# The odd mixer's operations in another order: scan beside value jobs, key copy in pieces, copies ahead of exponentials, turns in two banks

## The chip, the cores and the metric

One core of a Trainium2 chip runs the whole program. Times are device microseconds from start to end of one execution. TensorE (PE) multiplies, VectorE (DVE), ScalarE (ACT) and GpSimd (POOL) work on elements, and SyncE (SP) issues most of the DMAs. Every engine runs its own list of instructions in order, and semaphores alone order the engines against each other.

## The reference, cut to what matters

The program is a two-layer image-like block, then a two-layer sequence block on 512 tokens of width 1024, all in fp32: an even mixer, a feed-forward part, an odd mixer, a feed-forward part. The change lies in the odd mixer. It has two halves that do not depend on each other until the output product:

```python
def s5_group(u, ...):                      # 32 groups, 64 complex states
    bu = einsum('bsgh,gph->bsgp', u, b_bar)
    state = associative_scan(s5_combine, (a_bar, bu))   # h = a*h + b, over time
    y = gelu(real(einsum('bsgp,ghp->bsgh', state, cm)) + d_skip * u)
    return y * sigmoid(y @ w_glu + b_glu)

def mla_group(c_q, c_kv, k_rope, pos, ...):             # 8 heads
    q = (rms_norm(c_q) @ w_uq).reshape(b, s, 8, 64 + 32)   # 32 of them rotated
    kv = (rms_norm(c_kv) @ w_ukv).reshape(b, s, 8, 64 + 64)
    k_rot = rope(k_rope)                   # one for all 8 heads
    p = softmax((q_nope @ k_nope + q_rot @ k_rot) * scale, causal by chunks of 64)
    return p @ v
```

## The kernel before, in words

All of it is one straight program for each engine. For the odd mixer one list, `odd_program` (L336), gives the order of the jobs, and TensorE (L1687 on), ScalarE (`odd_mixer`, L2270 on) and VectorE (L3220 on) each walk this same list and do their own share of each job. So the list is the order of work on three engines at once.

The jobs: `uq i` multiplies the normalised query rank by the weights of head i (6 matmuls, L1313), ScalarE copies the 96 rows to `qm` (L2280). `swap i` multiplies head i by a permutation (L1701) into bank 5, and VectorE rotates the head with three operations (L3228 to L3230). `k7` makes the kernels of the S5 steps with 64 matmuls of 16 columns (L1705). `wt i` transposes four blocks of 128 by 128 (L1709), ScalarE copies them (L2282). `kn i` makes the unrotated key of head i, `v i` 128 tokens of values. `in i` feeds 8 groups of the S5 input through the transposed blocks (L1725). `rot1 i` and `rot2 i` are one matmul (L1732) and three VectorE operations each, ahead of and behind the scan (L3250), which VectorE does in one instruction after `rot1 3`. `out`, `ytr`, `glu` finish S5.

`unit u` is attention for one head and one query tile of 128 (32 units, a pair of heads side by side). In slot u of the list TensorE does the scores of unit u (L1646, banks 0 and 1 in turn), the turn of unit u-2 (transposes of the probabilities, L1656, into bank 4), and in even slots the product with the values (mix, L1669). VectorE does the maximum of unit u and the weighting of unit u-1. ScalarE does the exponential of unit u (L2253) and then the copy of the turned probabilities of unit u-2 (L2261). A turn waits for its weighted probabilities and for the copy of the turn ahead of it, since both use bank 4. An exponential waits for its maximum and for the turn of unit u-2. A copy waits for its turn and for the mix that last read its buffer. Scores of unit u wait for the exponential of unit u-2. From unit 28 on parts of the output product (`early`) stand between the units.

All the jobs other than the swaps and units use banks 2 and 3 in turn, and wait until the job two places ahead has been taken out of its bank.

Ahead of the mixer stands the input product (`od_in`, L1609): ten tiles of 24 matmuls, which VectorE takes out and between which it computes the S5 tables (`tables`, L3141). TensorE's swap of the key rope part (L1630) stands behind tile 6. VectorE's key rope (L3179 to L3181) stands behind the scaling of the query rank. At the end of this part VectorE copies the rotated key part to all 8 heads of `km` in one instruction (L3187). TensorE enters the mixer when the variance of the kv rank has been computed (L3155).

Of the kernel before, what the change touches and what calls it, by code (L numbers as in the profile page):

```python
# [335 lines left out]
def odd_program():  # L336

    some = lambda kind, *which: [(kind, i) for i in which]
    program = some("uq", 0, 1) + some("swap", 0) + some("uq", 2) + some("swap", 1) + some("uq", 3) + some("swap", 2)
    program += some("k7", 0) + some("wt", 0) + some("swap", 3) + some("wt", *range(1, 8))  # L340
    program += some("kn", *range(4)) + some("v", *range(4)) + some("in", *range(4))
    beside = {0: some("rot1", 0, 1), 1: some("rot1", 2, 3), 2: some("uq", 4), 3: some("uq", 5) + some("swap", 4), 4: some("uq", 6) + some("swap", 5),
              5: some("uq", 7) + some("swap", 6), 6: some("rot2", 0, 1) + some("swap", 7), 7: some("rot2", 2, 3), 8: some("kn", 4, 5), 9: some("kn", 6, 7),
              11: some("out", 0, 1), 12: some("out", 2, 3), 13: some("out", 4, 5), 14: some("out", 6, 7), 16: some("ytr", 0, 1), 17: some("ytr", 2, 3),
              20: some("glu", 0), 21: some("glu", 1), 22: some("glu", 2), 23: some("glu", 3)}
    for u in range(35):
        program += some("unit", u) + beside.get(u, []) + some("early", *range(2 * (u - EARLY_AT), 2 * (u - EARLY_AT) + 2) if u >= EARLY_AT else ())
    return program


SIDE = [item for item in odd_program() if item[0] in SIDE_BY]


# [17 lines left out]
def build(nc, xt, ctxt, cvec, pack1, pack_c, w_fnet, w_ada, w_in, w_br, w_merge, w_out,  # L371
          pos, pack2, s5_bc, ev_w_in, ev_w_out, od_w_in, w_glu, w_uq, w_ukv, od_w_out, ffn_gate, ffn_up, ffn_down, out):
    ctx = ExitStack()
    with ctx:
# [292 lines left out]
        od_ready = sem("od_ready")  # L667
        odd_done = sem("odd_done")
# [4 lines left out]
        kr_swapped = sem("kr_swapped")  # L673
# [231 lines left out]
        def _(pe):  # L905
# [703 lines left out]
            def od_in():  # L1609
                q0 = PANEL0["od_in"]  # L1610

                def sums(name, k_tiles, bank, freed):
                    pe.wait_ge(od_ready, freed)
                    for k in range(k_tiles):
                        pe.wait_ge(squared, NORM0[name] + k + 1)
                        mm(psum[:, bank * BANK:(bank + 1) * BANK], ones2, NORM_AT[name][0][:, k, :], start=k == 0, stop=k == k_tiles - 1).then_inc(summed, 1)

                for n, tile in enumerate(OD_TILES):
                    if n % 2 == 0:
                        w = split_ready(q0 + n // 2)  # L1620
                    if n >= 7:
                        pe.wait_ge(od_ready, max(1, n - 7))
                    split_job(n % 8, w, tile % 2 * P if tile < 9 else 64, h2_parts, each=norm_tile(4) if n == 0 else None).then_inc(gemm_done, 1)
                    if n == 0:
                        statistics("mix1")
                    if n == 5:
                        sums("q", 3, 2, 3)
                    if n == 6:
                        pe.wait_ge(od_ready, 6)
                        mm(psum[64:96, 4 * BANK:5 * BANK], c2("swap_mla")[64:96, 64:96], kr[64:96, :], start=True, stop=True).then_inc(kr_swapped, 1)  # L1630
                    if n == 7:
                        sums("kv", 2, 3, 4)

            def odd_mixer():
# [4 lines left out]
                def scores(u):  # L1639
                    h, i = units[u]  # L1640
                    pe.wait_ge(qm_roped, h + 1)
                    pe.wait_ge(side_freed["act"], side_evicted("kn", h))
# [6 lines left out]
                def turn(u):  # L1649
                    h, i = units[u]  # L1650
                    pe.wait_ge(p2_weighted, u0 + u + 1)
                    if u:
                        pe.wait_ge(p2T_ready, u0 + u)
                    for j in range(i + 1):
                        o = 4 * BANK + j * P
                        last = nc.tensor.transpose(psum[:, o:o + P], pr_mla[0][:, u % 2, j * P:(j + 1) * P], ident2)  # L1656
                    last.then_inc(turned2, 1)
# [28 lines left out]
                for what, i in odd_program():  # L1686
# [15 lines left out]
                    elif what == "k7":  # L1702
                        pe.wait_ge(wv_ready, 1)
# [3 lines left out]
                    elif what == "wt":  # L1707
                        for g in range(4):
# [84 lines left out]
        def _(act):  # L1793
# [449 lines left out]
            def odd_mixer():  # L2243
# [12 lines left out]
                def copy(u):  # L2256
# [4 lines left out]
                    f(pr_mla[1][:, u % 2, 0:n], psum[:, 4 * BANK:4 * BANK + n], ACT.Copy).then_inc(p2T_ready, 1)  # L2261
# [8 lines left out]
                for what, i in odd_program():  # L2270
# [8 lines left out]
                    if what == "uq":  # L2279
                        f(qm[0:96, i, :], src[0:96, :], ACT.Copy).then_inc(side_freed["act"], 1)  # L2280
                    elif what == "wt":
# [15 lines left out]
                    elif what == "unit":  # L2297
                        if i < len(units):
                            exps(i)
                        if 0 <= i - 2 < len(units):  # L2300
                            copy(i - 2)
# [29 lines left out]
        def _(dve):  # L2331
# [784 lines left out]
            def od_in():  # L3116
# [49 lines left out]
                for n in range(10):  # L3166
# [7 lines left out]
                    elif n == 7:  # L3174
                        low_rank_scale("q", cq, "q_norm")
                        dve.wait_ge(kr_swapped, 1)
# [4 lines left out]
                        order(tt(kr[p], kr[p], temp, ALU.add))  # L3181
# [5 lines left out]
                order(v.tensor_copy(km[64:96], kr[64:96].unsqueeze(1).broadcast_to([32, MLAH, SEQ])))  # L3187

            def odd_mixer():
# [29 lines left out]
                for what, i in odd_program():  # L3219
# [5 lines left out]
                    if what == "swap":  # L3225
                        r = slice(0, 96)
                        dve.wait_ge(qm_swapped, i + 1)
# [74 lines left out]
        def _(pool):  # L3302
# [74 lines left out]
            for t in range(4):  # L3377
                pool.wait_ge(od_ready, 7 + t)
# [189 lines left out]
```

## Time and profile before

| | us |
|---|---|
| median of 3 runs (lowest, highest) | 2979.51 (2977.66, 2985.71) |
| the profiled execution, its own time | 2982.23 |
| its span, first to last instruction | 2980.3 |
| TensorE busy | 2870.1 (96%) |
| VectorE, GpSimd, ScalarE busy | 1405.7, 1356.8, 851.6 |
| share of TensorE in the chain that ended last | 83% |

The span is what the profile sees; the execution's own time has 1.93 us more around it. A time in a row counts from the start of the span. The odd mixer lies at about 2352 to 2558.

### The profile page before, as it was taken

The numbers are of one execution on the slowest core, as the hardware profiler recorded it, in microseconds if no ns is written. First come the engines' busy times: TensorE is split into PE (matmuls) and PEld (weight loads), VectorE is DVE, ScalarE is ACT, GpSimd is POOL, SyncE is SP. The second block draws the span as 40 slices with busy tenths as digits, with TensorE's granted clock in tenths as the row PEclk, the third lists the DMA queues.
The fourth block names the chain that finished last, engine by engine and source line by source line (L and its number), as shares of the span: only waits on it lengthen the run. The fifth ranks groups of instructions, "written<-read, shape, count | busy, mean of one in ns | idle before, by whom it ended". The sixth has DMA issues, their size and how long they took to land.

```text
span 2980.3 us, 36560 instructions
## 1 busy us (share of the span) xinstructions
PE 2870.1 (96%) x14468; PEld 2202.2 (74%) x14468; DVE 1405.7 (47%) x2280; ACT 851.6 (29%) x1579; POOL 1356.8 (46%) x1106
## 2 busy tenths in 40 slices
PE   8999999999989999999999998999999888999997
PEld 5878777777878777677876666788787545788886
DVE  3311656766563123436755876525536854611113
ACT  3011432320130143323245243232233124322222
POOL 2334323223535544458754544744445211744443
PEclk9999999999999999999999999999999899999999
DMA  7112222223312212133211112323324200323322
GB/s 279 44 43 64 64 70 90 65 93 124 102 43 85 78 53 71 54 127 103 85 59 56 57 43 75 98 85 89 105 76 149 59 30 29 108 90 92 106 82 74
DMA packets 244820, 245.76 MB, mean 82 GB/s; under 512 B 5376, under 2 KB 234624, under 8 KB 244032
## 3 DMA queue, kind: packets, MB, share of 16 engines
q1 hardware_dynamic: 243360, 239.92, 25.2%
q0 software_dynamic: 1312, 3.80, 0.4%
q8 instruction: 101, 1.65, 0.2%
q14 instruction: 47, 0.39, 0.0%
HBM read 235.19 MB, written 7.34 MB: 81 GB/s over the span
## 4 chain that ended last, share of the span: by engine, by line
PE 83%; DVE 13%; ACT 2%; issue 1%; SPq 1%; POOL 0%; DMA 0%; DVEq 0%; ACTq 0%; POOLq 0%
PE psum L930 22%; PE psum L932 21%; PE psum L931 21%; PE psum L1196 4%; PE psum L1313 1%; PE psum L1175 1%; PE psum L1131 1%; DVE columns L2610 1%; PE psum L1086 1%; PE psum L1151 1%; PE psum L1130 1%; PE psum L1200 1%; PE psum L1386 1%; DVE columns L2881 1%; PE psum L1462 1%
## 5 line engine op out<-in xcount | busy, mean ns | idle before, releaser
L930 PE MATMUL psum<-columns,columns 128*128 128x512 f32 (+1 forms) x3464 | 1350.6, 390 | 13.2 <-POOL columns L3320 5.0
L932 PE MATMUL psum<-columns,columns 128*128 128x512 f32 (+1 forms) x3464 | 1265.3, 365 | 0.0
L931 PE MATMUL psum<-columns,columns 128*128 128x512 f32 (+1 forms) x3464 | 1263.1, 365 | 0.0
L3320 POOL TENSOR_TENSOR columns<-columns,columns 128x512 fp32r<-128x512 f32 (+1 forms) x676 | 912.2, 1380 | 436.3 <-ACT columns L1850 403.1
L3316 POOL TENSOR_TENSOR columns<-columns,columns 128x512 fp32r<-128x512 f32 x392 | 418.3, 1098 | 1066.3 <-PE psum L932 835.6
L930 PEld LDWEIGHTS psum<-columns,columns 128*128 128x128 f32 x3464 | 656.0, 189 | 194.9 <-issue 76.0
L931 PEld LDWEIGHTS psum<-columns,columns 128*128 128x128 f32 x3464 | 656.6, 190 | 125.6 <-issue 29.2
L932 PEld LDWEIGHTS psum<-columns,columns 128*128 128x128 f32 x3464 | 654.9, 189 | 111.7
L1850 ACT ACTIVATE columns<-columns 128x1024 fp32r<-128x1024 f32 (+2 forms) x154 | 136.8, 936 | 170.1 <-PE psum L932 165.8
L2610 DVE SCALAR_TENSOR_TENSOR columns<-columns,columns,columns 128x256 f32<-128x256 f32 x224 | 153.7, 740 | 0.0
L2592 DVE SCALAR_TENSOR_TENSOR columns<-columns,psum 128x512 f32<-128x512 f32 x80 | 54.7, 684 | 185.8 <-PE psum L1196 183.4
L2988 DVE TENSOR_TENSOR columns<-columns,psum 128x512 f32<-128x512 f32 x44 | 30.3, 689 | 207.2 <-PE psum L932 207.2
L1196 PE MATMUL psum<-columns,columns 128*128 128x512 f32 x256 | 120.4, 592 | 1.4 <-DVE columns L2569 1.4
L2982 DVE TENSOR_TENSOR columns<-psum,columns 128x512 f32<-128x512 f32 x44 | 30.4, 692 | 151.8 <-PE psum L932 151.5
L2551 DVE TENSOR_REDUCE columns<-psum 128x1 f32<-128x768 f32 (+3 forms) x80 | 61.5, 769 | 64.7 <-PE psum L1131 63.6
L3104 DVE TENSOR_TENSOR psum<-psum,columns 128x512 f32<-128x512 f32 x32 | 22.4, 700 | 129.2 <-PE psum L932 129.1
L1959 ACT ACTIVATE columns<-psum,columns 128x768 f32<-128x768 f32 (+3 forms) x80 | 59.4, 742 | 71.6 <-DVE columns L2554 71.5
L2189 ACT ACTIVATE columns<-columns 128x512 fp32r<-128x512 f32 x44 | 27.9, 633 | 179.0 <-DVE columns L2988 179.0
L1974 ACT ACTIVATE columns<-psum 128x512 f32<-128x512 f32 (+1 forms) x80 | 44.1, 551 | 113.4 <-PE psum L1151 113.4
L2000 ACT ACTIVATE columns<-psum,columns 128x512 f32<-128x512 f32 x64 | 43.7, 682 | 111.6 <-PE psum L932 111.5
L1966 ACT ACTIVATE columns<-columns,columns 128x768 f32<-128x768 f32 (+3 forms) x80 | 62.6, 783 | 45.2 <-DVE columns L2562 45.1
L2185 ACT ACTIVATE columns<-columns 128x512 f32<-128x512 f32 x44 | 27.8, 632 | 162.0 <-DVE columns L2982 161.8
(410 smaller groups left out, 2859.9 us busy)
## 6 DMA issues: line engine op xcount, KB each, us to landing
columns<-in_w_merge SPq DMA_DIRECT2D x32, 1024.0 KB, 6.3
columns<-in_w_ada SPq DMA_DIRECT2D x24, 1024.0 KB, 5.3
columns<-in_w_in SPq DMA_DIRECT2D x22, 1024.0 KB, 5.3
columns<-in_ev_w_in SPq DMA_DIRECT2D x22, 1024.0 KB, 5.2
columns<-in_ffn_gate SPq DMA_DIRECT2D x22, 1024.0 KB, 5.3
columns<-in_ffn_up SPq DMA_DIRECT2D x22, 1024.0 KB, 5.3
columns<-in_ffn_down SPq DMA_DIRECT2D x16, 768.0 KB, 4.7
columns<-in_ffn_down SPq DMA_DIRECT2D x16, 640.0 KB, 4.3
```

Of the source, the lines that this page charges most:

```text
L930: mm(dst, weights(0, k), moving(0, k), start=start and k == 0, stop=False)
L931: mm(dst, weights(0, k), moving(1, k), start=False, stop=False)
L932: last = mm(dst, weights(1, k), moving(0, k), start=False, stop=stop and k == k_tiles - 1)
L1196: last = mm(psum[:, o:o + SEQ], brs[:, n % 2, k, part * P:(part + 1) * P], gx[:, r, k, :], start=k == 0, stop=k == 1)
L1850: last = f(w_parts[0][:, (SPLITS[q] - 1) % 2, a:b], ring[:, raw_slot, a:b], ACT.Copy)
L1959: f(prob[:, u % 2, 0:n], psum[:, o:o + n], ACT.Exp, bias=cols[:, u % 2:u % 2 + 1], scale=0.125, accum_out=cols[:, 4 + u % 2:5 + u % 2]).th ...
L1966: f(prob[:, u % 2, 0:n], prob[:, u % 2, 0:n], ACT.Identity, scale=cols[:, 24 + u % 8:25 + u % 8]).then_inc(prob_weighed, 1)
L2551: order(v.tensor_reduce(top, psum[:, o:o + n], AX.X, ALU.max))
L2592: v.scalar_tensor_tensor(out=acc if j < quarter else g, in0=g, scalar=1.0, in1=y, op0=ALU.add, op1=ALU.mult).then_inc(merge_used, 1)
L2610: last = v.scalar_tensor_tensor(out=acc, in0=w, scalar=sil[:, k, b:b + 1], in1=acc, op0=ALU.mult, op1=ALU.add)
L3316: last = g.tensor_tensor(high[:, c], raw[:, c], zero.broadcast_to([P, c.stop - c.start]), ALU.add)
L3320: last = g.tensor_tensor(low[:, c], raw[:, c], high[:, c].bitcast(F32), ALU.subtract)
```

## The change

Seven edits, none of which adds or removes arithmetic:

- The list of jobs is written anew. Six of the eight transpose jobs stand among the first `uq` and `swap` jobs, ahead of `k7`; the other two, `swap 3` and the `in` jobs follow it. `kn` and `rot1` alternate, and the `v` jobs stand behind the last `rot1`, beside the scan. Units 0 to 3 have one `uq` and one `rot2` beside them, units 4 to 7 one `swap` and one `kn`, units 8 to 10 nothing. From unit 11 on the list is as it was.
- The key rope's swap on TensorE stands behind tile 7 instead of tile 6.
- The copy of the key part to 8 heads is taken from VectorE and made by ScalarE in four pieces of 32 by 1024, each behind one of the copies `uq` 0 to 3. Scores wait for their piece (`km_ready`).
- ScalarE's copy of unit u-2 stands ahead of the exponential of unit u.
- Turns from unit 9 on use banks 4 and 5 in turn, and wait for the copy two turns ahead.
- The wait for the S5 tables moves from `k7` to `wt 0`.
- Semaphore counts follow from these.

```diff
-    program = some("uq", 0, 1) + some("swap", 0) + some("uq", 2) + some("swap", 1) + some("uq", 3) + some("swap", 2)
-    program += some("k7", 0) + some("wt", 0) + some("swap", 3) + some("wt", *range(1, 8))
-    program += some("kn", *range(4)) + some("v", *range(4)) + some("in", *range(4))
-    beside = {0: some("rot1", 0, 1), 1: some("rot1", 2, 3), 2: some("uq", 4), 3: some("uq", 5) + some("swap", 4), 4: some("uq", 6) + some("swap", 5),
-              5: some("uq", 7) + some("swap", 6), 6: some("rot2", 0, 1) + some("swap", 7), 7: some("rot2", 2, 3), 8: some("kn", 4, 5), 9: some("kn", 6, 7),
+    program = some("uq", 0, 1, 2) + some("swap", 0) + some("uq", 3) + some("wt", 0, 1) + some("swap", 1) + some("wt", 2, 3, 4, 5)
+    program += some("swap", 2) + some("k7", 0) + some("wt", 6, 7) + some("swap", 3) + some("in", *range(4))
+    for n in range(4):
+        program += some("kn", n) + some("rot1", n)
+    program += some("v", *range(4))
+    beside = {0: some("uq", 4) + some("rot2", 0), 1: some("uq", 5) + some("rot2", 1), 2: some("uq", 6) + some("rot2", 2),
+              3: some("uq", 7) + some("rot2", 3), 4: some("swap", 4) + some("kn", 4), 5: some("swap", 5) + some("kn", 5),
+              6: some("swap", 6) + some("kn", 6), 7: some("swap", 7) + some("kn", 7),
...
+TURNS_APART = 9
+def turn_bank(u):
+    return 4 + (u % 2 if u >= TURNS_APART else 0)
...
+        km_ready = sem("km_ready")
...
-        kr_swapped = sem("kr_swapped")
...
-                    if n == 6:
+                    if n == 7:
...
-                        mm(psum[64:96, 4 * BANK:5 * BANK], c2("swap_mla")[64:96, 64:96], kr[64:96, :], start=True, stop=True).then_inc(kr_swapped, 1)
-                    if n == 7:
+                        mm(psum[64:96, 4 * BANK:5 * BANK], c2("swap_mla")[64:96, 64:96], kr[64:96, :], start=True, stop=True).then_inc(qm_swapped, 1)
...
+                    pe.wait_ge(km_ready, h // 2 + 1)
...
+                    if u == TURNS_APART:
+                        pe.wait_ge(qm_roped, MLAH)
...
-                        pe.wait_ge(p2T_ready, u0 + u)
+                        pe.wait_ge(p2T_ready, u0 + u - (u > TURNS_APART))
...
-                        o = 4 * BANK + j * P
+                        o = turn_bank(u) * BANK + j * P
...
-                        pe.wait_ge(wv_ready, 1)
...
+                        if i == 0:
+                            pe.wait_ge(wv_ready, 1)
...
-                    f(pr_mla[1][:, u % 2, 0:n], psum[:, 4 * BANK:4 * BANK + n], ACT.Copy).then_inc(p2T_ready, 1)
+                    o = turn_bank(u) * BANK
+                    f(pr_mla[1][:, u % 2, 0:n], psum[:, o:o + n], ACT.Copy).then_inc(p2T_ready, 1)
...
+                        if i == 0:
+                            act.wait_ge(od_ready, 9)
+                        if i < 4:
+                            f(km[64:96, 2 * i:2 * i + 2], kr[64:96].unsqueeze(1).broadcast_to([32, 2, SEQ]), ACT.Copy).then_inc(km_ready, 1)
...
+                        if 0 <= i - 2 < len(units):
+                            copy(i - 2)
...
-                        if 0 <= i - 2 < len(units):
-                            copy(i - 2)
...
-                        dve.wait_ge(kr_swapped, 1)
+                        dve.wait_ge(qm_swapped, 1)
...
-                        order(tt(kr[p], kr[p], temp, ALU.add))
+                        tt(kr[p], kr[p], temp, ALU.add).then_inc(od_ready, 1)
+                        dve.wait_ge(od_ready, 9)
...
-                order(v.tensor_copy(km[64:96], kr[64:96].unsqueeze(1).broadcast_to([32, MLAH, SEQ])))
...
-                        dve.wait_ge(qm_swapped, i + 1)
+                        dve.wait_ge(qm_swapped, i + 2)
...
-                pool.wait_ge(od_ready, 7 + t)
+                pool.wait_ge(od_ready, 7 + t + t // 2)
...
```

## Rows read from the trace of the kernel before

**Rows 1.** The page: the span.
```profile
span 2980.3 us, 36560 instructions
```

**Rows 2.** Busy us by stretch: PE, PEld, DVE, ACT, POOL; then PEclk, DMA share, GB/s.
```profile
2410.00:2468.00 58.00, 44.79 (x145) 19.64 (x146) 40.87 (x90) 14.76 (x38) 7.77 (x9) 0.88 0.13 40
...
2558.00:2620.00 62.00, 61.47 (x260) 48.73 (x261) 34.06 (x31) 18.62 (x27) 48.01 (x36) 1.00 0.33 103
```

**Rows 3.** Whom TensorE waited for from 2325 to 2558 (total us, times, longest).
```profile
PE psum L1656 <- ACT columns L2261: 20.6, 10, 5.8
...
PE psum L1630 <- DVE columns L3136: 3.7, 1, 3.7
PE psum L1732 <- DVE columns L3243: 2.2, 3, 1.1
```

**Rows 4.** TensorE in order of time: start us, us, what (L1313 products, L1701 swaps).
```profile
2352.24 5.31 PE L1313 MATMUL psum<-columns,columns 128*96 128x512 f32 x12
2357.39 1.02 PE L1701 MATMUL psum<-columns,columns 96*96 96x512 f32 x2
2358.25 2.74 PE L1313 MATMUL psum<-columns,columns 128*96 128x512 f32 x6
2365.47 1.99 PE L1701 MATMUL psum<-columns,columns 96*96 96x512 f32 x2 [4.47 <-DVE columns L3230]
2367.25 4.54 PE L1313 MATMUL psum<-columns,columns 128*96 128x512 f32 x6
```

**Rows 5.** VectorE in order of time: variance of kv, copy of keys, scan.
```profile
2350.36 0.68 DVE L3155 TENSOR_SCALAR columns<-psum 128x512 f32<-128x512 f32 x1
...
2360.87 2.28 DVE L3187 COPY columns<-columns 32x4096 f32<-32x4096 f32 x1
...
2420.83 4.42 DVE L3250 TENSOR_TENSOR_SCAN columns<-columns,columns 128x2048 f32<-128x2048 f32 x1
```

**Rows 6.** TensorE in order of time, units 1 to 11 (L1646 scores, L1656 turns).
```profile
2417.95 2.82 PE L1313 MATMUL psum<-columns,columns 128*96 128x512 f32 x6 [0.99 <-DVE columns L3243]
...
2427.00 0.45 PE L1656 MATMUL psum<-columns,columns 128*128 128x128 f32 x1 [5.80 <-ACT columns L2261]
2427.24 5.26 PE L1313 MATMUL psum<-columns,columns 128*96 128x512 f32 x6
...
2455.12 1.09 PE L1656 MATMUL psum<-columns,columns 128*128 128x128 f32 x4 [3.92 <-ACT columns L2261]
...
2457.47 4.67 PE L1313 MATMUL psum<-columns,columns 128*64 128x512 f32 x8
...
2462.92 3.65 PE L1313 MATMUL psum<-columns,columns 128*64 128x512 f32 x8
...
2468.26 0.70 PE L1646 MATMUL psum<-columns,columns 96*128 96x256 f32 x2
```

**Rows 7.** Groups by form, 2352 to 2558: busy us, mean ns, idle before.
```profile
L1646 PEld LDWEIGHTS psum<-columns,columns 96*128 96x128 f32 x64 | 11.5, 202 | 9.6 <-issue 9.2
...
L1725 PE MATMUL psum<-columns,columns 128*128 128x64 f32 x64 | 7.3, 274 | 0.0
...
L3228 DVE TENSOR_TENSOR columns<-psum,columns 96x512 f32<-96x512 f32 x8 | 5.5, 687 | 13.7 <-PE psum L1701 13.6
...
L2261 ACT ACTIVATE columns<-psum 128x512 f32<-128x512 f32 x8 | 4.7, 592 | 3.4 <-PE psum L1669 2.0 <-PE psum L1656 1.3
```

**Rows 8.** Groups by form of ScalarE: its copy of 1024 columns.
```profile
L1850 ACT ACTIVATE columns<-columns 128x1024 fp32r<-128x1024 f32 x122 | 123.6, 1048 | 170.1 <-PE psum L932 165.8 <-DMA columns<-in_od_w_in 4.3
```

**Rows 9.** TensorE in order of time: the two longest waits of turns behind unit 15.
```profile
2491.47 0.63 PE L1656 MATMUL psum<-columns,columns 128*128 128x128 f32 x4 [1.89 <-ACT columns L2261]
...
2531.16 0.98 PE L1656 MATMUL psum<-columns,columns 128*128 128x128 f32 x4 [3.02 <-ACT columns L2261]
```

**Rows 10.** Single microseconds in the kernels L1705 and transposes L1709, columns as rows 2.
```profile
2378.00:2379.00 1.00, 1.00 (x7) 1.00 (x6) 0.00 (x0) 0.00 (x0) 0.00 (x0) 0.50 0.00 0
2384.00:2385.00 1.00, 1.00 (x9) 0.98 (x7) 0.80 (x2) 0.18 (x1) 0.00 (x0) 0.74 0.00 0
```

## The prediction

> **What bounds the kernel now.** I read the page first: a span of 2980.3 us [rows 1], nearly all of it TensorE. So I looked for stretches where TensorE is not the bound, and the table by stretches shows them [rows 2]: behind the mixer TensorE is busy 61.5 of 62 us, in the 58 us of the mixer from 2410 on 44.8, at a mean granted clock of 0.88. Thus the mixer loses twice: TensorE waits, and behind a wait it runs for a while at 1.2 GHz and not at 2.4. The view of waits names the places [rows 3]: 20.6 us in ten turns that wait for ScalarE's copy, 3.7 us in the key rope's swap. The order of time shows the rest, one wait of 4.47 us for VectorE [rows 4] and two large ones at the turns, 5.80 and 3.92 us [rows 6].
>
> What a wait costs beside itself is read from pairs. A swap takes 1.02 us and six products 2.74 us; behind the wait of 4.47 us the same two take 1.99 and 4.54 us, 2.8 us more [rows 4]. Behind the wait of 5.80 us six products take 5.26 us, 2.5 us more [rows 6]. Behind the wait of 3.92 us eight products take 4.67 us against 3.65 us for eight at full clock, 1.0 us more, and the turn and mix ahead of them, 2.35 us from start to start (2455.12 to 2457.47), would take half of that at full clock, 1.2 us: together 2.2 us [rows 6].
>
> **The change part by part.** I work against the profiled execution and replay TensorE's list with these durations, as far as the start of unit 11, which is 2468.26 before [rows 6]. From there the list of jobs is the old one.
>
> *The start.* TensorE's 3.7 us of waiting at the key rope's swap [rows 3] goes, because tile 7 is multiplied during it. But this leads to nothing: TensorE enters the mixer only when VectorE has the variance of kv, which ends at 2350.36 + 0.68 = 2351.0 [rows 5], and VectorE works there without a gap, in the same order. TensorE came at 2352.24 [rows 4], so 1.1 us is won. TensorE will now be done some 5 us ahead of that time and stand idle, so the first products run at the low clock; I take the 2.8 us above. Net +1.7 us.
>
> *The key copy.* On VectorE it ran from 2360.87 for 2.28 us [rows 5], and the first head's rotation stood behind it; for that TensorE waited 4.47 us at the second swap [rows 4]. Now VectorE takes the first swap at once, and TensorE has `uq 2`, `uq 3` and two transpose jobs ahead of the second swap, over 6 us of work against 2.1 us of rotation (three operations of 0.687 us, rows of the form in [rows 7]). The wait and its low clock go: -4.5 - 2.8 = -7.3 us. On ScalarE a piece of 32 by 1024 has no row. From above it is the copy of 128 by 1024, 1.05 us [rows 8], from below the copy of 512 columns, 0.59 us [rows 7]. I take 1.05 us, because time goes by columns and not by partitions. It stands behind the release of the bank, so only the eviction behind it can be late: `wt 0` is, by about 1 us, and TensorE waits at `wt 2` for its bank. Those waits for ScalarE at the transposes come to 0.6 us more than before. Without that cover all four pieces would cost 4.2 us.
>
> *Rot1 and scan.* Before, units 0 to 3 held TensorE up for VectorE's rotations (2.2 us at L1732 [rows 3], of which I put 0.7 to unit 7 below, and 0.99 us ahead of `uq 4` [rows 6]), then for the scan of 4.42 us [rows 5], with the wait of 5.80 us behind it [rows 6]. Eight matmuls of 512 columns take 3.65 us [rows 6], so `kn` and `v`, of four, take 1.8 us, and `rot1`, of two, 0.9 us. Now `kn` and `rot1` alternate, 2.7 us of TensorE against 2.1 us of VectorE, so VectorE keeps up. The last rotation and the scan need 2.1 + 4.4 = 6.5 us beside four value jobs, 7.2 us. That is a cover with 0.7 us to spare; if it fails, unit 0's maximum is late but TensorE has `uq 4` to do. Gone: 1.5 + 1.0 + 5.8 and 2.5 us of low clock, -10.8 us.
>
> *Units 4 to 8.* The wait of 3.92 us, the 0.7 us ahead of it, and 2.2 us of low clock go, -6.8 us, because a unit has one swap and one `kn` beside it and no rotation of the scan. New here: VectorE comes into unit 4 some 2 us behind TensorE, since `rot2 3` is its last, and then has a maximum, a weighting and a rotation to do; `swap 5` must wait for the rotation of `swap 4` in the common bank, 1.3 us by my replay. Units 8 to 10 have nothing beside them, so each turn waits for weights; I find 0.7 us. Together +2.0 us.
>
> *Order behind k7.* TensorE falls to 1.2 GHz in the kernels of 16 columns (0.50 at 2378) and is back only in the transposes (0.74 at 2384) [rows 10]. Before, seven transpose jobs and fourteen us of dense products followed; now `wt 6`, `wt 7`, `swap 3` and `in` do. I take 1.0 us more at the low clock. Bounds: 0, and 9 us if the clock does not rise in the `in` jobs (a rival below).
>
> *Copies first, two banks, from unit 11 on.* Without beside work a turn no longer waits for a copy that stands behind an exponential. At unit 16 the turn waited 1.89 us and at unit 25 3.02 us [rows 9]. Nothing can be won below 0 or above these 4.9 us; the turn will wait for its weights instead, which VectorE finishes while the old copy runs (0.59 us [rows 7]), so I take one copy less at each and as much at unit 32, 1.9 us with the wait between engines. Against this, ScalarE's chain of table loads and activations in units 16 to 19 is as long as before. In even units the copy waits for the mix, so the exponential behind it comes later; I charge 0.9 us for both. Net -1.0 us.
>
> *Moved or added at nothing.* One more wait at each of 32 scores: between 0 and 0.3 us each (9.2 us of idle that only issue explains stand ahead of the 64 weight loads of the scores [rows 7], two to a score), I take 0, for these gaps lie under the matmul ahead. POOL's eight DMAs behind `in 3` and its clearing of the table come some 20 us earlier, and `out 0` needs them only in unit 11. POOL's stores wait for counts that name the same evictions. SP's panels wait for the products that free their slots, so they move ahead with them; at a DMA share of 0.13 [rows 2] nothing is in their way.
>
> Sum: 1.7 - 7.3 + 0.6 - 10.8 - 6.8 + 2.0 + 1.0 - 1.0 = -20.6 us. Behind the mixer TensorE is full [rows 2], so all of it reaches the end. The profiled execution took 2982.23 us and would take 2961.6. The median of the runs shown is 2979.51 us, 2.7 us below it; from that, 2958.9 us.
>
> The Trainium skill, TensorE: Matmul & The Clock Gate, Part 4: PE-mode transpose, says that transposes do not count as busy work for the clock the way matmuls do. By that rule the six transpose jobs ahead of `k7` would bring the clock down sooner. Here the clock rose while transposes ran, beside one swap [rows 10], so the trace does not bear it out, though it cannot exclude it.
>
> **The rivals.** (a) *The clock stays low from the transposes through `in`.* For it: two low stretches are already here, one inside `k7` [rows 10], and dense products no longer follow. Against it: the `in` jobs ran at full clock before. `in` takes 7.3 us [rows 7] and would take twice that; with `wt 6`, `wt 7` and a slower `k7` it is 9 us more: -12, 2967.5 us. The Trainium skill's rule on transposes, named above, would act this way.
>
> (b) *VectorE becomes the bound of units 0 to 10.* It was busy 40.9 of 58 us there [rows 2], and the same work now fits in some 39 us, beside TensorE's own. Each loop of bank, maximum, exponential, weights, turn then shows some wait. At 0.65 us a unit over eleven units, 7 us: -14, 2965.5 us.
>
> (c) *More is won.* The start stays at full clock (2.8 us), and the low stretches behind units 19 and 24, of 2 to 3 us each, vanish with their waits: -26, 2953.5 us. Against it: 3.02 us of wait shrink only to 2.5.
>
> (d) *The gain is given back behind unit 11*: some data of the output product comes at its old time. POOL splits the first panel behind `ytr`, which moves along, so little speaks for it. Gain 5: 2974.5 us.
>
> (e) *Slower: exponentials behind copies.* In each of 16 even units the exponential waits for the mix. At worst this is a mix at full length, 1.1 us, and a copy of 0.59 us [rows 7], 1.7 us times 16 = 27 us, against the 20.6 won: +6, 2985.5 us. It decides from 1.3 us a unit on. Against it: the exponential's maximum takes VectorE about as long as turn and mix take TensorE, so most of the delay is covered.
>
> **How the numbers follow.** Forecast 50 in 100, (a) 15, (b) 12, (c) 12, (d) 7, (e) 4. The predicted time is the forecast's, 2958.9 us; its own range, with the uncertain 2 to 4 us of new waits and clock, is 2954 to 2963. The range of 8 in 10 reaches over (a), (b) and (c) and the upper end of the added waits, 2951 to 2970. About 0.3%, 9 us, is what a measurement of this kernel tells from no change. Faster by more than that: forecast, (a), (b), (c), less a little for medians that drift, 0.88. Within it: (d), 0.07. Slower: (e) and mishaps with no name, 0.05.
>
> **What would show it.** In the trace after, the first mixer product should start near 2351 behind an idle stretch of 5 us and at clock 0.5; no wait of over 2 us should stand at the swaps or at the turns before unit 11; the scan should lie beside L1719; scores of unit 11 should start near 2447. `in` (L1725) should keep about 274 ns a matmul; 450 and more means (a). Many waits of L1656 or L1701 for VectorE in units 0 to 10 mean (b). If the step at unit 11 is there but not at the end of the mixer near 2537, it is (d) or (e). I am wrong at the root if the wait at the second swap or in unit 3 is still there, for then it was not the key copy or the scan that held them.

## The result and the profile after

The changed kernel takes 2967.37 us (median of five runs, 2960.47 to 2971.10), the kernel before 2979.51 (median of five, 2976.37 to 2985.71): a ratio of 0.9946, 95% interval 0.9932 to 0.996. The medians lie 12.1 us apart; the ratio, which is estimated from all the runs and is not the quotient of the two medians, stands for 16 us, and its interval for 12 to 20 us. The forecast was 20.6 us. So the sign and the range held, the size was too large, and rival (a) came nearest.

The profile below is of the slowest of the five executions (2971.10 us), so its parts describe that end.

The page of the changed kernel, its span, against [rows 1]:

```profile
span 2969.2 us, 36592 instructions
```

Busy us by stretch in the changed kernel, columns as in [rows 2], with the two stretches of there and five single microseconds from `k7` to the first `kn`, against [rows 10]:

```profile
2376.00:2377.00 1.00, 1.00 (x9) 1.00 (x8) 0.00 (x0) 0.00 (x0) 0.00 (x0) 0.68 0.00 0
2378.00:2379.00 1.00, 1.00 (x6) 1.00 (x7) 0.00 (x0) 0.00 (x0) 0.00 (x0) 0.50 0.00 0
...
2390.00:2391.00 1.00, 1.00 (x7) 1.00 (x7) 0.42 (x1) 0.00 (x0) 0.00 (x0) 0.50 0.00 0
...
2402.00:2403.00 1.00, 1.00 (x2) 0.23 (x1) 0.00 (x0) 0.37 (x1) 1.00 (x1) 0.50 0.00 0
...
2404.00:2405.00 1.00, 1.00 (x3) 0.30 (x2) 0.00 (x0) 0.39 (x1) 1.00 (x1) 1.00 0.00 0
2410.00:2468.00 58.00, 56.52 (x231) 27.60 (x231) 41.00 (x98) 23.18 (x56) 0.00 (x0) 1.00 0.13 46
2558.00:2620.00 62.00, 61.69 (x262) 48.81 (x261) 28.31 (x27) 18.92 (x25) 43.55 (x34) 1.00 0.32 102
```

The holes of 2410 to 2468 are filled: 56.52 of 58 us busy at clock 1.00, where it was 44.79 at 0.88 [rows 2]. But ahead of it TensorE is busy in every microsecond from 2377 to 2403 at 0.50, that is 1.2 GHz. The low stretch lasts 27.3 us, from 2376.4 to 2403.7. Before, the one that began in the same job lasted 6.8 us, from 2377.7 to 2384.5, and ended in the transposes [rows 10].

Whom TensorE waited for in the changed kernel from 2318 to 2558, against [rows 3]:

```profile
PE psum L1324 <- issue: 5.8, 1, 5.8
PE psum L1657 <- ACT columns L2267: 4.5, 2, 3.7
PE psum L1669 <- DVE columns L3232: 3.7, 3, 2.2
PE psum L1669 <- ACT columns L2276: 0.8, 2, 0.4
PE psum L1714 <- DVE columns L3249: 0.7, 1, 0.7
```

Turns (L1669, before L1656) waited 20.6 us for copies and now wait 0.8 us for them and 3.7 us for their weights. The first line is the idle time at the mixer's entry. The second and third lie behind unit 11 and are new.

TensorE in order of time in the changed kernel (start us, us, what, and in brackets the idle time ahead), against [rows 4] and [rows 6]:

```profile
2353.81 10.66 PE L1324 MATMUL psum<-columns,columns 128*96 128x512 f32 x18 [5.75 <-issue]
2364.30 1.02 PE L1714 MATMUL psum<-columns,columns 96*96 96x512 f32 x2
...
2369.08 1.02 PE L1714 MATMUL psum<-columns,columns 96*96 96x512 f32 x2
...
2373.48 11.04 PE L1717 MATMUL psum<-columns,columns 128*128 128x16 f32 x64
2384.36 2.13 PE L1723 MATMUL psum<-columns,columns 128*128 128x128 f32 x8
2386.28 1.91 PE L1714 MATMUL psum<-columns,columns 96*96 96x512 f32 x2
2387.98 13.75 PE L1739 MATMUL psum<-columns,columns 128*128 128x64 f32 x64
2401.67 2.91 PE L1324 MATMUL psum<-columns,columns 128*64 128x512 f32 x4
...
2405.56 1.93 PE L1324 MATMUL psum<-columns,columns 128*64 128x512 f32 x4
...
2414.22 7.16 PE L1733 MATMUL psum<-columns,columns 128*128 128x512 f32 x16
...
2442.54 1.07 PE L1714 MATMUL psum<-columns,columns 96*96 96x512 f32 x2 [0.70 <-DVE columns L3249]
...
2459.62 0.70 PE L1657 MATMUL psum<-columns,columns 96*128 96x256 f32 x2
```

The second swap (2369.08) has no wait ahead of it. `in` (L1739) takes 13.75 us. Scores of unit 11 start at 2459.62, 8.64 us earlier than before [rows 6]. VectorE's scan, in its order of time, lies inside the value jobs (L1733, 2414.22 to 2421.38):

```profile
2416.66 4.42 DVE L3269 TENSOR_TENSOR_SCAN columns<-columns,columns 128x2048 f32<-128x2048 f32 x1
```

To compare executions I cut each into five parts by its own events, since the time at which the sums of the q rank start (2317.53 before, 2320.12 after) moves from execution to execution, upstream of the change. "Low" is the time for which 1.2 GHz was granted, idle time of TensorE in it included; a us of it in which TensorE is busy costs half a us.

| | sums to mixer | mixer to scores of unit 11 | to the last mix | behind it | low to unit 11 | low from there to the last mix |
|---|---|---|---|---|---|---|
| before | 34.7 | 116.0 | 86.4 | 425.7 | 27.3 | 13.7 |
| after | 33.7 | 105.8 | 83.0 | 426.7 | 32.8 | 13.7 |

The spans differ by 11.1 us: +2.6 upstream, -1.0, -10.2 and -3.5 in the three parts, +1.0 behind. TensorE's idle time from the mixer's first product to unit 11 fell from 18.3 to 2.1 us, by 16.2; the low clock gave part of it back.

### The profile page after: what moved, and what is told of

It reads as the page before. It is cut to its first block, busy times and chain, and to the rows that moved or that the text cites. A ratio compares the mean times of both kernels' runs of the same rounds, so it can differ in the third digit from the quotient of the medians.

```text
span 2969.2 us, 36592 instructions
## 1 busy us (share of the span) xinstructions
PE 2876.1 (97%) x14468; PEld 2208.4 (74%) x14468; DVE 1402.0 (47%) x2279; ACT 857.0 (29%) x1583; POOL 1355.3 (46%) x1106
## 4 chain that ended last, share of the span: by engine, by line
PE 83%; DVE 12%; issue 2%; ACT 2%; POOL 1%; SPq 1%; DMA 0%; DVEq 0%; ACTq 0%; POOLq 0%
PE psum L941 21%; PE psum L943 20%; PE psum L942 20%; PE psum L1207 4%; PE psum L1324 2%; PE psum L1186 1%; PE psum L1142 1%; DVE columns L2629 1%; PE psum L1097 1%; PE psum L1162 1%; PE psum L1141 1%; POOL columns L3339 1%; PE psum L1211 1%; PE psum L1657 1%; DVE columns L2900 1%
```

## The experiments

Eleven kernels ran in three groups. Ratios are against the kernel before, run on the same chip beside them: its median was 2982.69 us beside e1 to e4, 2981.34 beside e5 to e8, 2979.93 beside e9 to e11. "Low behind" is the low time from unit 11 to the last mix.

| | median us | ratio, 95% interval | mixer to u11 | to last mix | low to u11 | low behind |
|---|---|---|---|---|---|---|
| e1_again | 2970.84 | 0.9949 (0.9936, 0.9963) | 105.8 | 83.0 | 32.9 | 13.7 |
| e2_kn_between_in | 2964.55 | 0.9936 (0.9923, 0.9949) | 103.3 | 82.7 | 19.5 | 13.7 |
| e3_old_list | 2974.12 | 0.9971 (0.996, 0.9982) | 112.6 | 83.0 | 29.3 | 13.7 |
| e4_dense | 2960.70 | 0.9926 (0.9913, 0.9938) | 101.0 | 81.6 | 19.5 | 6.8 |
| e5_dense_exp_first | 2960.99 | 0.9931 (0.9918, 0.9945) | 101.5 | 83.5 | 19.6 | 12.1 |
| e6_dense_one_bank | 2961.40 | 0.9931 (0.9917, 0.9944) | 101.0 | 81.6 | 19.5 | 6.8 |
| e7_dense_key_vector | 2959.80 | 0.9925 (0.9911, 0.9938) | 100.4 | 84.8 | 18.4 | 13.7 |
| e8_dense_early_rope | 2958.61 | 0.9922 (0.9908, 0.9935) | 96.4 | 84.8 | 10.2 | 13.7 |
| e9_dense_neither | 2967.31 | 0.9953 (0.9938, 0.9968) | 101.1 | 88.1 | 18.7 | 27.3 |
| e10_list_only | 2968.77 | 0.9957 (0.9941, 0.9973) | 106.5 | 86.0 | 30.7 | 20.5 |
| e11_k7_halves | 2958.76 | 0.9922 (0.9909, 0.9935) | 96.9 | 84.8 | 10.2 | 13.7 |

My theory for the missing 8 us was rival (a): the clock falls in `k7`, and nothing behind it brings it back before the first `kn`. Its rivals: new waits of VectorE (b), and a loss by the copies' order (e).

**e1_again.** The changed kernel, no edit.

> The changed kernel once more, nothing edited, as the yardstick of this call. Clock theory: the granted clock is 0.5 from inside k7 to the first kn job, the in jobs take about 13.8 us instead of 7.3, and the time is 12 to 16 us below the kernel before. Rival (the low stretch was an accident of one execution, the shortfall lies elsewhere): the in jobs take about 7.3 us and yet the time is no better than 12 us below before.

0.9949, and the same parts to 0.1 us. Its six runs spread over 13 us (2958.65 to 2971.75), more than most steps between these kernels; the mean granted clock of a run goes along (0.987 at 2958.65, 0.984 at 2966.5, 0.982 at 2970 and above). Differences of 2 to 3 us between kernels are read from the parts, not from medians. But the parts are one execution of each kernel, and both profiles of the changed kernel are of slow ones (2971.10 and 2970.18). Its fastest run, 2958.65, equals the fastest of e4_dense, 2958.47, all five of which ran at 0.988; whether the long low stretch is there in such a run, no trace shows.

**e2_kn_between_in.** Dense products of 512 columns between the `in` jobs.

```diff
-    program += ... + some("in", *range(4))
     for n in range(4):
-        program += some("kn", n) + some("rot1", n)
+        program += some("kn", n) + some("in", n)
+    program += some("rot1", *range(4))
```

> The changed kernel with kn 0 to 3 between the in jobs, and rot1 0 to 3 in a row behind them. Clock theory: dense products return right behind swap 3, so the clock is back at 1.0 by in 1 or in 2, the in jobs take 8 to 10 us, some 5 to 6 us are won; the four rot1 now wait for VectorE, 3 x 1.2 = 4 us, so the whole is 1 to 3 us faster than the changed kernel. Rival (clock costs nothing here, since these jobs are bound by weight loads): in jobs take as long as in the changed kernel or the time is 4 us longer than it.

Low fell from 32.9 to 19.5 us and the four `in` jobs took 2.00 us each. The part won only 2.5 us, because the rotations now stand in a row and TensorE waits for VectorE between them, 3.0 us in all (order of time, this kernel):

```profile
2402.35 1.13 PE L1747 MATMUL psum<-columns,columns 128*128 128x512 f32 x2 [0.68 <-DVE columns L3263]
2404.52 1.13 PE L1747 MATMUL psum<-columns,columns 128*128 128x512 f32 x2 [1.05 <-DVE columns L3263]
2406.70 1.98 PE L1734 MATMUL psum<-columns,columns 128*128 128x512 f32 x4 [1.05 <-DVE columns L3263]
```

**e4_dense.** The same, with a value job behind each `rot1`, and `rot2` one unit later.

```diff
-    program += some("rot1", *range(4))
-    program += some("v", *range(4))
+    for n in range(4):
+        program += some("rot1", n) + some("v", n)
-    beside = {0: some("uq", 4) + some("rot2", 0), 1: ...
+    beside = {0: some("uq", 4), 1: some("uq", 5) + some("rot2", 0), ...
```

> The changed kernel with kn n and in n in turn, then rot1 n and v n in turn, and each rot2 one unit later (the last one in unit 4). Clock theory: the in jobs take 8 to 10 us, VectorE is covered at each rot1, the scan has v 3, unit 0 and uq 4 as cover, 4.4 + 2.1 us against about 5; 4 to 8 us faster than the changed kernel, 18 to 23 below before. Rival: the scan is uncovered by 2 to 4 us and the clock returns late, no faster than the changed kernel.

The waits in `rot1` are gone (one of 1.13 us for ScalarE ahead of `rot2 0` came instead), the part is 101.0 us, and the whole is 0.9926 where the unedited kernel had 0.9949. Order of time, this kernel, from `k7` on:

```profile
2370.29 10.86 PE L1718 MATMUL psum<-columns,columns 128*128 128x16 f32 x64
2380.98 2.13 PE L1724 MATMUL psum<-columns,columns 128*128 128x128 f32 x8
2382.90 1.92 PE L1715 MATMUL psum<-columns,columns 96*96 96x512 f32 x2
2384.75 3.04 PE L1325 MATMUL psum<-columns,columns 128*64 128x512 f32 x4
2387.72 2.00 PE L1740 MATMUL psum<-columns,columns 128*128 128x64 f32 x16
2389.65 1.93 PE L1325 MATMUL psum<-columns,columns 128*64 128x512 f32 x4
```

The granted clock is low from 2373 to 2387 and back in the first `kn` (3.04 us, the second 1.93); `in` then takes 2.00 us for 16 matmuls where the changed kernel takes 13.75 for 64. So rival (a) is shown for the profiled executions, and it is the order behind `k7` that decides how long the clock stays low.

**e3_old_list.** The changed kernel with the list of before: key copy in pieces, copies first, two banks and the late key rope alone.

```diff
-    program = some("uq", 0, 1, 2) + some("swap", 0) + ...
+    program = some("uq", 0, 1) + some("swap", 0) + some("uq", 2) + ...
```

> The changed kernel with the list of jobs of before; key copy on ScalarE, copies ahead of exponentials, two banks and the later key rope swap stay. Clock theory: the in jobs are back at 7.3 us, the wait at the second swap is gone (the key copy is), the waits of 5.8 and 3.9 us at the turns shrink only a little; time 5 to 9 us below before. Rival (the list is not what brings the gain): as fast as the changed kernel or faster, 12 us and more below before.

Order of time, this kernel, the entry, the second swap and the two large turns:

```profile
2353.99 8.03 PE L1321 MATMUL psum<-columns,columns 128*96 128x512 f32 x12 [5.79 <-issue]
...
2365.87 1.07 PE L1711 MATMUL psum<-columns,columns 96*96 96x512 f32 x2 [0.41 <-DVE columns L3246]
...
2427.07 0.48 PE L1666 MATMUL psum<-columns,columns 128*128 128x128 f32 x1 [5.34 <-DVE columns L3229]
...
2453.86 0.66 PE L1666 MATMUL psum<-columns,columns 128*128 128x128 f32 x4 [3.23 <-DVE columns L3229]
```

VectorE in order of time, this kernel: the end of the scaling of the kv rank and the start on the first head:

```profile
2362.27 1.42 DVE L3178 SCALAR_TENSOR_TENSOR columns<-columns,columns,columns 128x512 f32<-128x512 f32 x2
2363.60 0.68 DVE L3244 TENSOR_TENSOR columns<-psum,columns 96x512 f32<-96x512 f32 x1
```

Without the list the wait at the second swap still shrinks from 4.47 to 0.41 us, but not by the key copy alone. VectorE starts on the first head right behind the scaling of the kv rank in place of 2.3 us later; the other 1.7 us are TensorE's own delay, for it enters 1.0 us earlier and then takes 8.03 us for the first twelve products where it took 5.31 [rows 4]. The scan's waits stay (5.80 to 5.34, 3.92 to 3.23 [rows 6]). Their releaser is now named as VectorE and not ScalarE: with the copy first, the turn of unit 1 waits for its own weighting, which VectorE does behind the scan and the maximum of unit 2. The part behind unit 11 is 83.0 us, as in the changed kernel.

**e10_list_only.** The kernel before with the new list and nothing else.

```diff
-    program = some("uq", 0, 1) + some("swap", 0) + some("uq", 2) + ...
+    program = some("uq", 0, 1, 2) + some("swap", 0) + ...
```

> The kernel before with the new list of jobs and nothing else: key copy by VectorE, key rope behind tile 6, exponentials first, one bank. If the list is what brings the gain: as fast as the changed kernel or 1 to 3 us faster, since TensorE comes to the mixer without a wait; 12 to 18 us below before, the in jobs at low clock or not as the clock falls. My prediction's account (7.3 us for the key copy) would have it 5 us and more slower than the changed kernel, with a wait of over 2 us at the second swap.

0.9957 against 0.9946 and 0.9949 of the whole change, intervals that overlap. The key copy on VectorE, with the list and a start at full clock, leaves a wait of 1.19 us at the second swap. 106.5 us to unit 11 against 105.8, and 86.0 behind it against 83.0. The list is worth nearly all of the part to unit 11, and copies and banks the 3 us behind it, with the old list (86.4 to 83.0) as with the new. These 3 us are not made alike: with the old list TensorE waits 10.9 us behind unit 11 without the two edits and 8.4 with them, at 13.7 us low both times; with the new list it waits 8.1 and 8.4 us, and what falls is the low time, from 20.5 to 13.7 us.

**e5_dense_exp_first, e6_dense_one_bank, e9_dense_neither.** From e4_dense: the exponential ahead of the copy again (e5), all turns in one bank (e6), both (e9).

```diff
-                        if 0 <= i - 2 < len(units):
-                            copy(i - 2)
                         if i < len(units):
                             exps(i)
+                        if 0 <= i - 2 < len(units):
+                            copy(i - 2)
```
```diff
-TURNS_APART = 9
+TURNS_APART = 99
```

> The order of e4_dense (kn and in in turn, rot1 and v in turn) with the exponential of unit u ahead of the copy of unit u-2 again, as before. My prediction's term: from unit 11 on the copies first win 1 us, and in units 0 to 10 little, so 1 to 2 us slower than e4_dense, and turns wait for copies again at units 16 and 25 (1.9 and 3.0 us). Rival (copies first win the 3.5 us that the changed kernel's trace shows behind unit 11): 3 to 5 us slower. Rival (exponentials behind copies cost): faster than e4_dense.

> The order of e4_dense with all turns in bank 4. If copies first do the work, a turn finds its bank free anyway: within 1 us of e4_dense. If the second bank does it: 2 to 4 us slower, with turns that wait for copies from unit 11 on.

> The order of e4_dense with both edits behind unit 11 undone: exponential ahead of copy, all turns in bank 4. The profiles so far have 86.4 us from the scores of unit 11 to the last mix before, and 81.6 to 84.8 with either edit alone or both. If each of the two edits is enough to take a turn off the wait for a copy, undoing both brings back waits of about 2 and 3 us for copies at units 16 and 25 and 86 us, 2 to 4 us slower than e4_dense. Rival (the 3 us come from the phase of the clock): within 1 us of e4_dense.

Either alone costs nothing that can be told (0.9931 and 0.9931 against 0.9926), both together 7 to 8 us (0.9953, six runs from 2962.47 to 2973.27): in time the two are substitutes. In e9 the part behind unit 11 is 88.1 us with 27.3 low, in e4 81.6 us with 6.8 low. Whom TensorE waits for there, in e9 (from 2470 to 2550) and then in e4 (from 2460 to 2560, the two largest):

```profile
PE psum L1670 <- ACT columns L2277: 7.3, 6, 3.0
...
PE psum L1670 <- DVE columns L3233: 4.6, 4, 2.2
PE psum L1658 <- ACT columns L2268: 4.5, 2, 3.7
```

So e9 does not wait longer but less, 7.3 us against 9.3. It is slower because 26.2 us of its matmuls there ran at 1.2 GHz against 6.8 us in e4. Half of that difference, 9.7 us, less the 2.0 us of waiting, makes 7.7 us, where the parts differ by 6.5; 1.2 us stay unassigned. The expectation had put 2 to 4 us down to the waits that come back; they did come back, in place of others as long, and the loss is the clock's. Why the clock is low for longer there, no run here shows. By the parts e6 equals e4 to 0.1 us, and e5 is 1.9 us longer at the same waits of 9.3 us, with 12.1 us low against 6.8.

**e7_dense_key_vector.** From e4_dense: the key copy back on VectorE in one instruction.

```diff
-                        if i < 4:
-                            f(km[64:96, 2 * i:2 * i + 2], kr[64:96]...broadcast_to([32, 2, SEQ]), ACT.Copy)
+                v.tensor_copy(km[64:96], kr[64:96]...broadcast_to([32, MLAH, SEQ])).then_inc(km_ready, 1)
```

> The order of e4_dense with the key part copied to 8 heads by VectorE in one instruction again. Since the list has uq 2, uq 3 and two transposes ahead of the second swap, my account puts the wait of 4.5 us down to copy and list together: the copy moves VectorE's first swap by 2.3 us, the cover is 6 us against 4.4, so 0 to 1 us slower. Rival (the copy alone made that wait): a wait of 2 to 4 us at the second swap and 4 to 7 us slower with its low clock.

100.4 us to unit 11 against 101.0, 0.9925 against 0.9926: with three `uq` ahead of the first swap, and `uq 3` and two transposes ahead of the second, the list covers the copy of 2.28 us [rows 5] when TensorE also enters late and at the low clock, as here. Moving it was not needed for that; with a start at full clock e10_list_only puts what it saves at 1.19 us.

**e8_dense_early_rope.** From e4_dense: the key rope's swap behind tile 6 again.

```diff
-                    if n == 7:
+                    if n == 6:
                         pe.wait_ge(od_ready, 6)
                         mm(psum[64:96, 4 * BANK:5 * BANK], ...).then_inc(qm_swapped, 1)
+                    if n == 7:
```

> The order of e4_dense with the key rope's swap behind tile 6 again, so that TensorE waits about 3.7 us there. VectorE is the bound of that part, so this wait costs nothing, and TensorE comes to the mixer without the idle of 5.8 us and at full clock: 2 to 3 us faster than e4_dense, first product of the mixer at clock 1.0. Rival (the idle ahead of the mixer costs nothing beside itself): within 1 us of e4_dense.

Order of time, this kernel: the key rope's swap, the first products, `k7`, the first `kn`:

```profile
2326.98 1.91 PE L1642 MATMUL psum<-columns,columns 32*32 32x512 f32 x2 [3.73 <-DVE columns L3157]
...
2349.11 7.89 PE L1325 MATMUL psum<-columns,columns 128*96 128x512 f32 x18
...
2366.01 9.92 PE L1719 MATMUL psum<-columns,columns 128*128 128x16 f32 x64
...
2379.53 2.33 PE L1325 MATMUL psum<-columns,columns 128*64 128x512 f32 x4
```

The wait of 3.73 us is back in the input product, the idle time at the entry is gone, and the first 18 products take 7.89 us where e4_dense takes 10.86. The mixer is entered 0.5 us later after the sums (34.2 against 33.7), the part to unit 11 is 4.6 us shorter: 3.0 in the first products, 0.9 in `k7` and 0.7 in the first `kn`. So the change's late key rope is a loss of about 4 us by the parts. The whole shows less, 0.9922 against 0.9926, which the intervals do not tell apart. In the two profiled executions the part behind unit 11 differs the other way by 3.2 us, and that is the clock again (low 13.7 against 6.8, waits 9.5 against 9.3); why it differs, and whether it does in the other runs, is open. With e11_k7_halves it is the fastest version found: 2958.61 us against 2981.34 of the kernel before beside it, and 2967 to 2971 of the changed kernel.

**e11_k7_halves.** From e8: `k7` in two halves of 32 matmuls with a swap and a `kn` between them, transposes apart.

```diff
-    program += some("swap", 2) + some("k7", 0) + some("wt", 6, 7) + some("swap", 3)
+    program += some("k7", 0) + some("swap", 2) + some("kn", 0) + some("k7", 1) + some("kn", 1) + some("wt", 4, 5) + some("swap", 3) + some("wt", 6, 7)
```

> The order of e8_dense_early_rope with k7 in two halves of 32 matmuls and a swap and kn jobs between and behind them, the eight transpose jobs spread among them. Clock theory: the stretch at the low clock around k7, 10 us in e8, shrinks to under 4 us, k7 takes 2 x 3.6 instead of 11 us, and the time is 3 to 5 us below e8_dense_early_rope. Rival (k7 is bound by its weight loads at either clock, so the clock costs nothing there): within 1 us of it.

A miss. Order of time, this kernel:

```profile
2364.67 4.02 PE L1720 MATMUL psum<-columns,columns 128*128 128x16 f32 x32 [0.20 <-ACT columns L2304]
2368.53 2.00 PE L1715 MATMUL psum<-columns,columns 96*96 96x512 f32 x2
2370.46 3.68 PE L1324 MATMUL psum<-columns,columns 128*64 128x512 f32 x4
2374.07 4.09 PE L1720 MATMUL psum<-columns,columns 128*128 128x16 f32 x32
2378.09 3.57 PE L1324 MATMUL psum<-columns,columns 128*64 128x512 f32 x4
```

The halves take 8.1 us together where `k7` took 9.92, but each is followed by a low stretch of its own (2368.0 to 2374.8 and 2378.2 to 2381.6), 10.2 us in all as in e8, and the swap and both `kn` pay for it.

## Why the prediction was right in its direction and wrong in its size

**The start** (+1.7): right, +1.8 us. First product 33.7 us after the sums and not 34.7, behind 5.75 us of idle time, and 2.8 us more for 18 products. e8 shows that this term was a loss that could be left out; (c), a start at full clock, did not occur.

**The key copy** (-7.3) and the transposes (+0.6): the wait and the low clock behind it went. A piece of 32 by 1024 takes ScalarE 1.05 us, the upper bound that was taken. The transposes wait 0.63 us, before 0.7, so the 0.6 was not due. But e7 and e10 show that the list without the move takes all of that wait, or all but 1.19 us of it: the term belongs for the most part to the list. The working had two slips here. It set `uq 2` between the first and the second swap, where only `uq 3` and the transposes stand, 4 us of cover and not 6. And it let VectorE take the first swap at once, though VectorE is done with the kv rank only at 2360.87 [rows 5], 2.5 us behind the end of that swap [rows 4]. That the wait went entirely also owes to the late start at the low clock.

**Rot1, scan, units 4 to 8** (-10.8 and -6.8): right. No such wait is left, and e3 shows that they stay without the list. New waits there (+2.0) were 0.70 at swap 5 and 0.77 at two turns, 1.5 us. The scores of unit 11 started at 2459.62, not near 2447.

**Order behind k7** (+1.0): this is the step that failed. In the kernel before (order of time) `k7`, the swap behind it and `in` were:

```profile
2372.49 8.93 PE L1705 MATMUL psum<-columns,columns 128*128 128x16 f32 x64
...
2382.14 1.91 PE L1701 MATMUL psum<-columns,columns 96*96 96x512 f32 x2
...
2402.72 7.25 PE L1725 MATMUL psum<-columns,columns 128*128 128x64 f32 x64
```

The low stretch lasted 27.3 us where it had lasted 6.8, all of it under busy matmuls: 20.5 us more at half the clock, 10.2 us where 1.0 stood. Term by term: `k7` 11.04 us against 8.93, 2.1 more; the first `kn` 2.91 and not 1.93, 1.0 more; `in` 13.75 against 7.25, 6.5 more; the transposes 0.3 more; the swap behind `k7` nothing, since it ran low before too (1.91 us both times). That is 9.9 us. The sign that I had set for (a), 450 ns a matmul in `in`, was nearly reached: 419 ns against 274. I had read from one row, clock 0.74 at 2384 among transposes [rows 10], that the clock would come back there in any order. After the change it did not come back in two transpose jobs, a swap and 64 `in` matmuls; it came back in the first dense `kn`. Before the change `in` ran at full clock because it was entered at full clock, behind `kn` and `v`. The bound of 9 us of that step, and rival (a), came close to it; the 15 in 100 I gave it was too little, and the argument "the `in` jobs ran at full clock before" held only where the job was entered at full clock. That the median, 2967.37 us, lies on rival (a)'s 2967.5 is luck in part: waits and copies gave 4 us more than forecast, and 3.6 us upstream of the mixer and behind it went the other way. On the rule of the Trainium skill, TensorE: Matmul & The Clock Gate, Part 4: PE-mode transpose, that transposes don't count as matmuls do for the clock: after the change the clock stayed low through two transpose jobs, which would fit it, and before it rose in them, which doesn't; no run here takes the transposes alone, so it stays open. The place where the clock fell doesn't settle it either: 2.9 us into `k7` in the changed kernel and 4.1 us in e8, both with six transpose jobs ahead of `k7`, 5.2 us before and 2.8 us in e3, both with none.

**Copies first and two banks** (-1.0): -3.5, right in sign. The waits of 1.89 and 3.02 us [rows 9] for copies went. What came in their place are a wait of unit 20's scores for an exponential and of a turn for its weights (TensorE in order of time, changed kernel):

```profile
2493.92 1.62 PE L1657 MATMUL psum<-columns,columns 96*128 96x384 f32 x2 [3.70 <-ACT columns L2267]
...
2519.96 1.11 PE L1669 MATMUL psum<-columns,columns 128*128 128x128 f32 x4 [2.18 <-DVE columns L3232]
```

Both are long, but the eight waits of turns for copies behind unit 11 (10.9 us, of which I had counted the two longest) became six of 8.4 us. That is 2.5 us of the 3.5; 0.6 us more is clock (11.9 us of matmuls at 1.2 GHz against 13.1). The mechanism is not shown by this alone: in e9 and e10, without both edits, the waits are shorter than in e4 and the changed kernel, and the time goes to the clock. Rival (e) does not decide: with the exponential ahead again (e5) the same two waits stand, 2.6 and 2.7 us, so the order of the two costs about a microsecond at one unit.

**The end.** From the last mix on nothing changed but 1.0 us, and that is clock (2.1 us of matmuls at 1.2 GHz that ran at 2.4 before), so (d) did not occur. (b) did not: waits for VectorE to unit 11 are 0.70 us. In sum, against the forecast of -20.6: the clock behind `k7` +9.2 (10.2 where 1.0 stood), new waits and transposes -1.4, copies and banks -2.5, and 0.6 us unassigned make -14.7; with the 1.0 behind the mixer -13.7, and with the 2.6 upstream of it the 11.1 us between the two spans.

## What to carry to other kernels

When an order of work is rewritten to remove waits, write down for each job at which granted clock it will start, not only what it waits for: here 16 us of waits went and about 10 came back as the same matmuls at half rate. Put dense products of 512 columns right behind a job of narrow matmuls (e2, e4), but do not expect more of cutting that job in two (e11), and let an unavoidable wait fall where long dense work follows in which the clock recovers, rather than at the entry of the stage. And of two cures for one wait (the order of two instructions, a second bank) try one alone: either gave the whole time here. Then look at waits and low clock apart, for the kernel with neither cure waited less and was slower.

## What the runs showed of the hardware

- TensorE was busy without a gap and still fell to 1.2 GHz in the 64 matmuls of 16 columns (`k7`), 2.3 (e5) to 5.2 us (before) into them, in every kernel; in halves of 32 (e11) near each half's end. It came back in 512-column products, but with the old list (before, e3) in transposes beside a swap, and in e11 once at the start of the second half.
- 64 matmuls of 64 columns (`in`) kept the clock at which they were entered: 7.25 us before, 13.75 us after.
- One program's time on one chip (e1) spread over 13 us (2958.65 to 2971.75), with its mean granted clock from 0.987 to 0.982.
- A copy of 32 by 1024 on ScalarE takes 1053 ns, one of 128 by 1024 1048 [rows 8]: fewer partitions saved nothing (the form's row, changed kernel).

```profile
L2299 ACT ACTIVATE columns<-columns 32x1024 f32<-32x1024 f32 x4 | 4.2, 1053 | 0.1
```
